# The delta rule's inversion in two pairs of chunks, with all projections of a level behind the second pair

## What is computed

```
a_mat = where(strict, einsum('nbhid,nbhjd->nbhij', kb, k) * decay, 0)
t_mat = triangular_solve(a_mat, eye, left_side=True, lower=True, unit_diagonal=True)
u = t_mat @ (v * beta);   w = t_mat @ (kb * exp(gc))
```

## Time and profile before

| | |
|---|---|
| median of 3 runs | 2868.02 us (2866.92 to 2870.99) |
| the profiled execution | 2871.3 us, its span 2869.5 us |
| mean granted TensorE clock | 0.988 of full speed |
| TensorE matmul records | 2763.4 us busy (96% of the span) |
| weight loads | 2201.5 us (77%) |
| VectorE, ScalarE, GpSimd | 1009.7, 1095.4, 1386.6 us (35, 38, 48%) |
| the eight heads of the delta rule | from about 1390 to 1789 us of the span |

### The profile page before, as it was taken

The page is one execution under the profiler, slowest core; times in us unless marked ns, Lnnn a source line. Parts: engine busy times, 40 slices in busy tenths (PEclk is TensorE's granted clock), DMA queues, the critical chain, the costliest instruction groups (busy, mean ns, idle before and its releaser), DMA issues.

```text
span 2869.5 us, 37353 instructions
## 1 busy us (share of the span) xinstructions
PE 2763.4 (96%) x14674; PEld 2201.5 (77%) x14674; DVE 1009.7 (35%) x1900; ACT 1095.4 (38%) x1641; POOL 1386.6 (48%) x1073
## 2 busy tenths in 40 slices
PE   7999899999989999999899998999999999899999
PEld 5977678888756788887677776888887977688887
DVE  3035431113485512214566664311122044522112
ACT  4255442224446523324334434422334355533221
POOL 3467544445455355444343442545445466544443
PEclk8999999999999999999999999999999999999999
DMA  4331122333422132324111110232323322123232
GB/s 123 94 83 52 45 89 89 102 102 88 103 44 75 59 100 92 100 90 111 45 45 45 35 55 16 88 98 94 101 88 95 96 66 67 45 89 98 92 102 73
DMA packets 271884, 227.81 MB, mean 79 GB/s; under 512 B 29205, under 2 KB 259349, under 8 KB 271749
## 3 DMA queue, kind: packets, MB, share of 16 engines
q1 hardware_dynamic: 260880, 216.29, 24.8%
q10 hardware_dynamic: 10868, 9.66, 1.4%
HBM read 223.62 MB, written 2.30 MB: 79 GB/s over the span
## 4 chain that ended last, share of the span: by engine, by line
PE 87%; DVE 6%; ACT 3%; POOL 2%; issue 1%; DMA 0%; ACTq 0%; DVEq 0%; POOLq 0%
PE bank L1764 49%; PE bank L1673 17%; PE bank L1825 5%; PE bank L2051 2%; PE bank L1800 2%; PE bank L2142 2%; POOL w_lo L556 1%; PE bank L1718 1%; PE bank L1876 1%; PE bank L1892 1%; POOL arena L579 1%; PE bank L2090 1%; PE bank L1978 1%; PE bank L1862 1%; PE bank L1906 1%
## 5 line engine op out<-in xcount | busy, mean ns | idle before, releaser
L556 POOL TENSOR_TENSOR w_lo<-raw,w_hi 128x512 fp32r<-128x512 f32 x808 | 1068.6, 1352 | 1216.2 <-ACT w_hi L699 1216.2
L699 ACT ACTIVATE w_hi<-raw 128x2048 fp32r<-128x2048 f32 x202 | 385.5, 1908 | 458.0 <-PE bank L1764 423.3
L1764 PE MATMUL bank<-h_hi,w_hi 128*128 128x512 f32 x1024 | 400.8, 391 | 0.0
L1764 PE MATMUL bank<-h_hi,w_lo 128*128 128x512 f32 x1024 | 398.4, 389 | 0.0
L1764 PE MATMUL bank<-h_lo,w_hi 128*128 128x512 f32 x1024 | 398.4, 389 | 0.0
L1764 PE MATMUL bank<-g_hi,w_hi 128*128 128x512 f32 x1024 | 398.3, 389 | 0.0
L1764 PE MATMUL bank<-g_lo,w_hi 128*128 128x512 f32 x1024 | 398.3, 389 | 0.0
L1764 PE MATMUL bank<-g_hi,w_lo 128*128 128x512 f32 x1024 | 398.3, 389 | 0.0
L1673 PE MATMUL bank<-h_hi,w_hi 128*128 128x512 f32 x776 | 325.1, 419 | 7.2 <-POOL w_lo L556 7.2
L1673 PE MATMUL bank<-h_lo,w_hi 128*128 128x512 f32 x776 | 316.7, 408 | 0.0
L1673 PE MATMUL bank<-h_hi,w_lo 128*128 128x512 f32 x776 | 313.7, 404 | 0.0
(11 more groups left out here) (253 smaller groups left out, 3851.2 us busy)
## 6 DMA issues: line engine op xcount, KB each, us to landing
raw<-in_mlp_w SPq DMA_DIRECT2D x128, 1024.0 KB, 5.2
raw<-in_a_w_in SPq DMA_DIRECT2D x48, 512.0 KB, 5.1
raw<-in_c_w_in SPq DMA_DIRECT2D x32, 512.0 KB, 5.4
raw<-in_a_w_in SPq DMA_DIRECT2D x12, 1024.0 KB, 5.1
raw<-in_b_w_in SPq DMA_DIRECT2D x18, 256.0 KB, 4.2
raw<-in_a_w_out SPq DMA_DIRECT2D x4, 1024.0 KB, 4.9
raw<-in_b_w_in SPq DMA_DIRECT2D x4, 1024.0 KB, 5.4
arena<-bias_scratch ACTq DMA_DIRECT2D x16, 256.0 KB, 3.4
```

The costliest lines, as they stand in the source:

```text
L556: ins = nc.gpsimd.tensor_tensor(w_lo[s][:, k, :], raw[s][:, k, :], w_hi[s][:, k, :].bitcast(F32), ALU.subtract)
L699: nc.scalar.activation(w_hi[s][:], raw[s][:], ACT.Copy).then_inc(w_hi_done, 1)
L1764: mm = nc.tensor.matmul(lin_bank[j][:], w[s][:, c, P * j:P * j + P], a[:, c, :], start=c + z == 0, stop=c == CT - 1 and z == 2)
```

## The change

The levels of the inversion run in two pairs of chunks, z = 0 (chunks 0 and 1) and z = 1 (chunks 2 and 3). W of a pair goes to a bank of its own (3 or 4), and so do the results of T and U of a pair (6 or 7; `packed` puts T's in the first 128 columns, U's in the next). ScalarE copies each half by itself, VectorE subtracts each half by itself, and the semaphores `w_done`, `w_copied`, `tw_done`, `t_done` and `u_done` count by pairs. At level 1, W also waits for the scaled keys, since bank 4 held them. `FILL_W[k]` becomes 38 + 7k - 7, which is where the level before had ended: there is no filler between W and the products of T and U any more, and all 7 come behind the second pair's. `FILL_TW` stays.

```diff
-        def packed(bank_k, k):
-
-            return bank[bank_k][:, 0:NB * 64].rearrange("p (c b s) -> p c b s", c=NB, s=1 << k)
+        def of_pair(m, z):
+
+            return m[:, 2 * z:2 * z + 2]
+
+        def w_half(z):
+
+            return bank[3 + z][:, 0:2 * P].rearrange("p (c n) -> p c n", c=2)
+
+        def packed(second, k, z):
+
+            return bank[6 + z][:, P * second:P * second + P].rearrange("p (c b s) -> p c b s", c=2, s=1 << k)
...
-        FILL_W = {k: 38 + 7 * k - 4 for k in range(1, LEVELS)}
+        FILL_W = {k: 38 + 7 * k - 7 for k in range(1, LEVELS)}
...
                         if k > 3:
-                            pool.wait_ge(w_done, 6 * h + k - 3)
+                            pool.wait_ge(w_done, 2 * (6 * h + k - 3))
...
                     for k in range(1, LEVELS):
-                        act.wait_ge(w_done, 6 * h + k)
-                        nc.scalar.activation(Wm, bk4(3), ACT.Copy).then_inc(w_copied, 1)
+                        for z in range(2):
+                            act.wait_ge(w_done, 2 * (6 * h + k - 1) + z + 1)
+                            nc.scalar.activation(of_pair(Wm, z), w_half(z), ACT.Copy).then_inc(w_copied, 1)
                         if k == 2 and nxt:
                             round_ahead(n1 + 2 * h + 2)
...
                     for k in range(1, LEVELS):
-                        dve.wait_ge(tw_done, 6 * h + k)
-                        if k < LEVELS - 1:
-                            a = halves_of(Tm, k, False)
-                            nc.vector.tensor_tensor(a, a, packed(6, k), ALU.subtract).then_inc(t_done, 1)
-                        a = halves_of(Um, k, True)
-                        nc.vector.tensor_tensor(a, a, packed(7, k), ALU.subtract).then_inc(u_done, 1)
+                        for z in range(2):
+                            dve.wait_ge(tw_done, 2 * (6 * h + k - 1) + z + 1)
+                            if k < LEVELS - 1:
+                                a = of_pair(halves_of(Tm, k, False), z)
+                                nc.vector.tensor_tensor(a, a, packed(False, k, z), ALU.subtract).then_inc(t_done, 1)
+                            a = of_pair(halves_of(Um, k, True), z)
+                            nc.vector.tensor_tensor(a, a, packed(True, k, z), ALU.subtract).then_inc(u_done, 1)
...
                     for k in range(1, LEVELS):
 
-                        if k == 1:
-                            pe.wait_ge(t_init, h + 1)
-                        else:
-                            pe.wait_ge(t_done, 5 * h + k - 1)
                         pe.wait_ge(atl_done, 6 * h + k)
-                        for c in range(NB):
-                            mm = nc.tensor.matmul(bk4(3)[:, c, :], atl[k % 3][:, c, :], Tm[:, c, :], start=True, stop=True)
-                        mm.then_inc(w_done, 1)
+                        for z in range(2):
+                            if k == 1:
+                                pe.wait_ge(t_init, h + 1)
+                                pe.wait_ge(kv_scaled, h + 1)
+                            else:
+                                pe.wait_ge(t_done, 10 * h + 2 * (k - 2) + z + 1)
+                            for c in (2 * z, 2 * z + 1):
+                                mm = nc.tensor.matmul(w_half(z)[:, c % 2, :], atl[k % 3][:, c, :], Tm[:, c, :], start=True, stop=True)
+                            mm.then_inc(w_done, 1)
                         filler(FILL_W[k])
-                        pe.wait_ge(w_copied, 6 * h + k)
-                        pe.wait_ge(u_done, 7 * h + k)
                         if k == 1:
                             pe.wait_ge(qkd_done, h + 1)
-                        for c in range(NB):
-                            if k < LEVELS - 1:
-                                in_halves(packed(6, k)[:, c], Um[:, c, :], halves_of(Wm, k, False)[:, c],
-                                                 start=True, stop=True)
-                        for c in range(NB):
-                            mm = in_halves(packed(7, k)[:, c], Wm[:, c, :], halves_of(Um, k, True)[:, c],
-                                                  start=True, stop=True)
-                        mm.then_inc(tw_done, 1)
+                        for z in range(2):
+                            pe.wait_ge(w_copied, 2 * (6 * h + k - 1) + z + 1)
+                            pe.wait_ge(u_done, 13 * h + 1 + (2 * (k - 2) + z + 1 if k > 1 else 0))
+                            for c in (2 * z, 2 * z + 1):
+                                if k < LEVELS - 1:
+                                    in_halves(packed(False, k, z)[:, c % 2], Um[:, c, :], halves_of(Wm, k, False)[:, c],
+                                              start=True, stop=True)
+                            for c in (2 * z, 2 * z + 1):
+                                mm = in_halves(packed(True, k, z)[:, c % 2], Wm[:, c, :], halves_of(Um, k, True)[:, c],
+                                               start=True, stop=True)
+                            mm.then_inc(tw_done, 1)
                         filler(FILL_TW[k])
```

## The result

The changed kernel takes 2876.41 us (median of 10 runs, 2873.74 to 2878.77) against 2869.24 us for the kernel before in as many runs beside it: ratio 1.0023, 95% interval 1.0015 to 1.0032. That is 7.2 us more (4.3 to 9.2 by the interval). The changed kernel is slower beyond the noise. The forecast was 2871.4 us, +3.4, with 2864 to 2880 as the range. The profiled execution took 2873.74 us, the fastest of the ten, with a span of 2871.9 us and a mean granted clock of 0.992.

A forecast was written before the change was run, and what follows sets the result against it. TensorE's own instruction order was taken as the bound (87% of the span). Terms +1.4 (levels 1 to 5), +1.2 (level 6), +3.5 (late rounding), -2.7 (last head) give +3.4 on 2868.0: 2871.4 us, range 2864 to 2880.

The forecast's parts named there:

- Start of the T and U products, levels 2, 4, 5: Inner heads: products start 1.07 to 1.12 us after W, level 3.90 us; +0.04 a level, +1.4 us over levels 1 to 5.
- Rival 2: Inner levels: second pair hides the first half copy, no stop left, level 3.62 us, kernel 2861 us; chance 0.08.
- rival 1: Seams between pairs cost TensorE a weight load each, 0.14 to 0.24 us a level, kernel near 2879 us; chance 0.17.
- The price of nothing for waits already fulfilled: TensorE's added waits that are already fulfilled cost 0; at 0.03 us the T and U seam would cost 1.3 us.
- The rounding: ScalarE's rounding of the next weights starts 3.2 us into level 2, delaying level 3's copy 0.5 us; seven heads, +3.5 us.
- Rival 3: The rounding isn't late (starts sooner, or copies pass it), so the change does nothing, 2868 us; chance 0.13.
- Level 6: Only U products there, so a second stop before the second copy is seen: 3.56 against 3.38 us, seven times, +1.2 us.
- The last head: Few projections there, so its levels gain: levels 2 to 5 take 2.97 instead of 3.52 us; together -2.7 us.
- the bound of 0.2%: Whole kernel: smallest difference a run can tell from no change, 5.7 us; bounds 2862.3 and 2873.8 us.
- the case of 0.33: Whole kernel measured slower, above 2873.8 us; chance 0.33.
- the case of 0.57: Whole kernel measured the same, between 2862.3 and 2873.8 us; chance 0.57.
- the 0.15 us of the earlier trace as a stop: Kernel before, ahead of a level's T and U products: TensorE stands still 0.15 us, waiting for ScalarE's copy of W.

The follow-up runs named there:

- the runs with cover: Changed kernel with projections put back between W and the T and U products: three a level, 2867.45 us; one (three in level 2), 2866.00 us.
- 8 useless products: Kernel before, without pairs, plus eight repeated matmuls in head 3 whose results nothing reads: 2873.78 us, +3.90 over the kernel before beside it.
- the version with all seven projections behind: Kernel before, without pairs (one copy of all four chunks), with all seven projections behind T and U: 2900.65 us, ratio 1.0110.

## Why the prediction was right, and where it wasn't

- **Start of the T and U products, levels 2, 4, 5:** forecast 1.07 to 1.12 us, 1.08 measured; levels 3.88 to 3.93 forecast, 3.89 measured. Rival 2 (no stop left, levels of 3.62) and rival 1 (a weight load for each seam, levels above 4.0) fall with this row. The price of nothing for waits already fulfilled holds there. At level 1, where more waits stand ahead of the first pair, it may not: +0.10 us instead of +0.04, seven times +0.4, cause open.
- **The rounding:** forecast to start at 3.2 us and to delay level 3 by 0.5; 3.22 and 0.49 (4.38 against 3.89) measured, 3.43 us of stage in the run that moves it. Rival 3 falls. The strict order that the Trainium skill states for ScalarE's queue (TensorE: Matmul & The Clock Gate, "Architectural detail: the array is 16× 32×32, not 1× 128×128") is what the trace shows: the copy due at about 1608.75 starts at 1609.26.
- **Level 6:** the second stop came where it was forecast, but the term was too small: +0.26 instead of +0.18. The second half's products were put at 0.305 us, half of a run without stop. The second copy ends at 1621.73; with the 0.05 us until it is seen, 0.38 us are left up to the projection at 1622.16.
- **The last head:** -2.7 forecast, -2.7 measured. That these agree to a tenth is luck: level 1 there runs partly at the granted clock 0.50 and took 4.38 us here, but 3.89 to 4.81 in the runs that leave this head as it is. Its levels 2 to 5 take 2.96 to 2.98 us (forecast 2.97):

```profile
1759.36 1.05 PE L2154 MATMUL bank<-arena 128*128 128x128 f32 x8
...
1762.34 1.05 PE L2154 MATMUL bank<-arena 128*128 128x128 f32 x8
...
1765.30 0.38 PE L2154 MATMUL bank<-arena 128*128 128x128 f32 x2
```

- **The sum:** +4.1 in the stage against +3.4; the two mis-sized terms make it up: 7 x 0.08 at level 6 and 7 x 0.06 at level 1 are 1.0, and the other levels came 0.2 to 0.3 lower.
- **The step that failed** is none of these. The prediction took the sum over the stage for the sum over the kernel: it has no term for the work behind, only 1.5 us for the runs' spread. The rest didn't stay as it was: +2.6 us in the profiles, of which 1.6 are shown at the start of layer 3. With it the median lies above the bound of 0.2%, the case of 0.33, and not within it, the case of 0.57, though the stage was forecast within 0.7 us. That 2876.4 us lies inside the range is luck in part: the upper part of the range stood for dearer seams (rival 1), which didn't come.
- **A misreading without effect:** the 0.15 us of the earlier trace rows as a stop. The sum went by absolute starts, which hold that time whatever it is called. As an argument for a gain it would have misled, as it did in the expectations of the runs with cover.

## What to carry to other kernels

Splitting a producer and its copy in two shortens a wait, but only work issued between them hides it: keep some filler there, and move the surplus to places where the view of waits shows TensorE standing. When fillers are shifted, look up every instruction on other engines that waits for one of them by number, here a rounding queued ahead of a copy on the critical path. For changes of a few microseconds, compare what lies behind the changed stage as well: it moved by 2.6 us here, and by as much with 8 useless products that lengthened the stage by 0.6.

## What the hardware showed beside this

- At one place of layer 3 a stretch at the granted clock 0.50 costs nothing on work ahead of a wait for VectorE, and 1.6 us behind it. Three pairs of versions whose stages agree within 0.5 us are alike in this; two at 375.71 and 376.29 us of stage, which ends some 400 us ahead of that place, are not.
- The change from projections of 512 columns to the products of 64 columns takes about 0.10 us with nothing waited for.
- The granted clock stayed at 1.00 with 0.69 us of a level of 4.55 us bare, in the inner heads of the version with all seven projections behind.
